# Second layer, latent attention: the division of the probabilities on GpSimd instead of VectorE

## The reference, cut to what matters

```python
def causal_attention(q, k, v):            # blocks of 128 queries
    sc = einsum('bqhd,bkhd->bhqk', q_blk, k) * scale
    sc = where(mask, sc, -inf)
    p = softmax(sc, axis=-1)
    return einsum('bhqk,bkhd->bqhd', p, v)

def memory_attention(q, mem_k, mem_v):
    sc = einsum('bshd,bmhd->bhsm', q, mem_k) / sqrt(HEAD_DIM)
    p = softmax(sc, axis=-1)
    return einsum('bhsm,bmhd->bshd', p, mem_v)

tok = causal_attention(q, k, v)
mem_out = memory_attention(q_mem, mem_kv[:, :, 0], mem_kv[:, :, 1])
y = concatenate([tok, mem_out], axis=-1) * silu(gate)
h = layer_norm(ALPHA * h + y @ w_out[layer], ln_g[layer], ln_b[layer])
```

## Time and profile before

| | us |
|---|---|
| runs of the kernel before, median (lowest to highest) | 3575.22 (3570.03 to 3576.9) |
| profiled execution, span | 3578.9 |
| PE busy | 3274.2 (91%) |
| PE weight loads busy | 2587.5 (72%) |
| DVE busy | 1949.7 (54%) |
| POOL busy | 1561.2 (44%) |
| ACT busy | 1156.5 (32%) |

### The profile page before, as it was taken

One profiled execution on the slowest core, in us unless ns is written; L12 is line 12 of the kernel. 1 busy time (PEld: TensorE's weight loads), 2 busy tenths in 40 slices (PEclk: granted clock), 3 DMA queues, 4 the chain that ended last, 5 costly groups with the idle time before them and its releaser, 6 DMA issues. The chain is left out here.

```text
span 3578.9 us, 45809 instructions
## 1 busy us (share of the span) xinstructions
PE 3274.2 (91%) x17652; PEld 2587.5 (72%) x17652; DVE 1949.7 (54%) x2824; ACT 1156.5 (32%) x2265; POOL 1561.2 (44%) x1195
## 2 busy tenths in 40 slices
PE   5888999999699999889999999999897999899796
PEld 2666787788598888667788878887674566676465
DVE  3278854545444455587733373338413887665736
ACT  4144432333333333332211021102223664144713
POOL 1114645455143441156666666666551001554332
PEclk9988869999899999899999999999996999999887
DMA  4335536232253442343333333334434321222112
GB/s 166 89 106 165 154 118 185 86 83 83 69 140 98 122 125 65 105 144 94 89 94 100 95 89 100 94 100 104 141 101 119 79 60 50 83 81 59 47 52 72
DMA packets 524317, 358.55 MB, mean 100 GB/s; under 512 B 92497, under 2 KB 477382, under 8 KB 524102
## 3 DMA queue, kind: packets, MB, share of 16 engines
q1 hardware_dynamic: 513446, 325.22, 31.6%
q0 software_dynamic: 4608, 16.78, 1.5%
q10 hardware_dynamic: 6048, 13.63, 1.1%
HBM read 276.85 MB, written 78.18 MB: 99 GB/s over the span
## 5 line engine op out<-in xcount | busy, mean ns | idle before, releaser
L2403 PE MATMUL psum<-place,place 128*128 128x512 f32 x2126 | 862.7, 406 | 80.5 <-POOL place L2381 33.5
L2404 PE MATMUL psum<-place,place 128*128 128x512 f32 x2126 | 843.1, 397 | 0.0
L2405 PE MATMUL psum<-place,place 128*128 128x512 f32 x2126 | 841.0, 396 | 0.0
L2379 POOL CAST place<-place 128x1024 fp32r<-128x1024 f32 (+3 forms) x302 | 304.7, 1009 | 1119.9 <-PE psum L2405 674.8
L2381 POOL TENSOR_TENSOR place<-place,place 128x1024 fp32r<-128x1024 f32 (+3 forms) x302 | 691.3, 2289 | 24.2
L2403 PEld LDWEIGHTS psum<-place,place 128*128 128x128 f32 x2126 | 408.7, 192 | 197.9 <-POOL place L2381 51.8
L2404 PEld LDWEIGHTS psum<-place,place 128*128 128x128 f32 x2126 | 408.9, 192 | 90.3 <-issue 7.5
L2405 PEld LDWEIGHTS psum<-place,place 128*128 128x128 f32 x2126 | 408.3, 192 | 87.6
L659 PE MATMUL psum<-place,place 128*128 128x512 f32 (+1 forms) x712 | 289.0, 406 | 22.1 <-issue 10.5
L660 PE MATMUL psum<-place,place 128*128 128x512 f32 (+1 forms) x712 | 273.7, 384 | 0.0
L661 PE MATMUL psum<-place,place 128*128 128x512 f32 (+1 forms) x712 | 273.5, 384 | 0.0
(11 more groups left out here) (325 smaller groups left out, 5592.1 us busy)
## 6 DMA issues: line engine op xcount, KB each, us to landing
place<-in_w_mlp_up SPq DMA_DIRECT2D x64, 512.0 KB, 4.0
place<-in_w_mlp_down SPq DMA_DIRECT2D x64, 512.0 KB, 3.9
place<-in_w_out SPq DMA_DIRECT2D x48, 512.0 KB, 4.0
chunked<-place SPq DMA_DIRECT2D x64, 320.0 KB, 3.6
place<-in_w_in SPq DMA_DIRECT2D x34, 512.0 KB, 5.8
solve<-in_w_ada POOLq DMA_DIRECT2D x32, 512.0 KB, 6.2
place<-in_lru_w_in SPq DMA_DIRECT2D x32, 512.0 KB, 3.8
place<-in_mla_w_in SPq DMA_DIRECT2D x30, 512.0 KB, 4.2
```

The costliest lines, as they stand in the source:

```text
L2379: nc.gpsimd.tensor_copy(hi, raw).then_inc(self.w_split, 1)
L2403: pe.matmul(ps, self.w_hi[:, j, k, :], hi, start=(k == 0), stop=False)
L2404: pe.matmul(ps, self.w_hi[:, j, k, :], lo, start=False, stop=False)
L2405: mm = pe.matmul(ps, self.w_lo[:, j, k, :], hi, start=False, stop=(k == kt - 1))
```

## The change

The half units' multiplication moves from DVE to POOL; DVE keeps the reciprocal, and waits before it until POOL has multiplied g - 2, since the reciprocals have two places. POOL's program in `rest` becomes: the multiplications of g = 0 to 111; the first two splits of the chain's weights; the multiplications of g = 112 to 127; then the chain's splits as before. `Recall` keeps the multiplication on DVE.

```diff
     DEPTH = PV = 2
+    POOL_DIVIDES = True
...
+    def gpsimd(self, pool):
+        for g in range(self.G):
+            p, rd = self.prob[:, g % 2, 0:self.blocks(g // 2) * P], self.st[g % 2][:, 3:4]
+            pool.wait_ge(self.rden, g + 1)
+            self.C.nc.gpsimd.tensor_scalar(p, p, rd, None, ALU.mult).then_inc(self.probs, 1)
+            yield
...
             dve.wait_ge(self.exped, g + 1)
+            if self.POOL_DIVIDES and g >= 2:
+                dve.wait_ge(self.probs, g - 1)
             nc.vector.reciprocal(rd, tot).then_inc(self.rden, 1)
-            dve.wait_ge(self.rden, g + 1)
-            ts(p, p, rd, None, ALU.mult).then_inc(self.probs, 1)
+            if not self.POOL_DIVIDES:
+                dve.wait_ge(self.rden, g + 1)
+                ts(p, p, rd, None, ALU.mult).then_inc(self.probs, 1)
...
     DEPTH = PV = 1
+    POOL_DIVIDES = False
...
         def _(pool):
-            alternate(only(LIN, HELD), chain.gpsimd(pool), None, None, None, None, lru.clear(pool))
+            division, weights = a.gpsimd(pool), chain.gpsimd(pool)
+            for g in range(a.G):
+                if g == a.G - 16:
+                    next(weights)
+                next(division)
+            alternate(only(LIN, HELD)[1:], weights, None, None, None, None, lru.clear(pool))
```

## The result

| | before | after |
|---|---|---|
| median of the runs, us | 3575.89 (3570.03 to 3576.9) | 3627.4 (3624.16 to 3636.06) |
| ratio after to before, 95% interval | | 1.0166 (1.0132 to 1.0199) |
| profiled execution, span, us | 3578.9 | 3634.2 |
| DVE busy, us | 1949.7 | 1894.2 |
| POOL busy, us | 1561.2 | 1760.4 |

The kernel is 51.5 us slower by the medians, 47 to 71 us by the interval of the ratio, where I forecast +2 us; the time lies above my range, which ended at 3597. DVE lost 55.5 us of work; POOL got 199.2 us more, where DVE had needed some 64 for the same multiplications.

A forecast was written before the change was run, and what follows sets the result against it. PE was taken to bound the kernel. From the profiled 3578.9 us, 0.0 for relief and lateness, -1.6 for the collision and +3.5 for the stall gave 3580.8; on the median, 3577 us, range 3571 to 3597.

The forecast's parts named there:

- What bounds the kernel: Latent pairs: PE sets the pace, busy 35.65 of 38.02 us, so edits elsewhere can win at most 2.37 us a pair.
- Part 1: Multiplication leaves DVE in latent pairs: about 8 us of DVE work freed a pair, but only 0 to 0.3 us credited.
- Part 2: GpSimd's multiplication priced like its cast, 1.04 us at 1024 columns; lateness and relief together zero, -0.3 to +0.5 us a pair.
- slack: Time from a division's end to its first transpose's weight load; 0.49 us at n = 8 (key blocks), second head.
- the middle case: Rival, also the middle price: GpSimd takes 1.72 us for 1024 columns, 2.2 us a pair lost; +16, 3591 us; chance 0.24.
- the subtraction's price: Rival: GpSimd's multiplication costs as much as its two-tensor subtraction, about 6.7 us a pair; +46, 3621 us; chance 0.10.
- Part 3: Sixth latent pair: GpSimd's splits no longer collide with a DVE division, 39.62 to 38.02 us, a gain of 1.6 us.
- Part 4: Start of last memory pair: two splits queued ahead of g = 112's division stall PE 3.5 us, bounded by 2.5 and 4.5.

The follow-up runs named there:

- e1: Changed kernel with POOL's multiplication replaced by a copy of the probabilities onto themselves, division left out, waits and order kept: 1.0060 of before, 3595.17 us.
- e7: e1 with the two weight splits taken apart, the first before g = 112, the second behind the last g: 1.0001 of before.
- e3: Changed kernel with POOL multiplying by the constant 0.5 instead of the column of reciprocals, division left out: 1.0154 of before.
- e4: Kernel before, division still on DVE, with GpSimd's first two weight splits held until the division of g = 111 is done: 1.0003 of before.
- e6: e4 with DVE's multiplication of g = 112 held until the two splits are done, all multiplications on DVE: 1.0064 of before.
- e5: Changed kernel with both weight splits moved behind all divisions, multiplication on POOL at full price: 1.0154 of before.
- e9: Changed kernel with the n = 8 multiplications back on DVE and the splits apart as in e7: 1.0089 of before.

## Why the prediction was wrong, point by point

- **What bounds the kernel.** Right. PE sets the pace, and 2.37 us of idle time a pair were all there was to win; none was won.
- **Part 1, the relief of DVE.** Right: DVE's share of a latent pair fell from 31.33 to 23.75 us, and with the price of the copy the pair lasted 38.08 us where it had lasted 38.02. I had put relief and lateness together at zero, from -0.3 to +0.5.
- **Part 2, the price.** This is the step that failed first. I took the cast's 1.04 us for 1024 columns because both read one tensor; the multiplication takes 2.85, above the upper bound of 2.41 from the subtraction. I had written that both ends stay in the range, and then left the upper one out of it. With 1.04 the latent pairs do what I said (e1, e7). The reading of slack was sound in the main: it said that n = 8 loses from about 1.2 us on, and at 1.89 us a pair lost 1.8 us, at n = 2, 3, 4 and 8 (the middle case gave 2.2 for 1.72). For the subtraction's price it gave 6.7 us a pair; e3, dearer still, shows 5.9 at full clock, so my sum was too high there, and which of its terms was is not shown. The rule of the Trainium skill (GPSIMD Engine Reference, section 4.1) that one input is roughly line-rate holds here for the copy (1.04 us at 1024 columns, against 0.753 on DVE) and not for the multiplication by a scalar (2.85 us). The warning of the same section against elementwise work on GpSimd was the better guide.
- **Part 3, the collision.** Right to 0.1 us: 39.62 to 38.02 (e4), 38.09 (e1). L1728 (L1739 after) was not stretched:

```profile
L1739 DVE TENSOR_TENSOR place<-place,place 128x512 fp32r<-128x512 f32 x16 | 11.1, 693 | 19.6 <-ACT place L1784 19.6
```

  By the rule of the Trainium skill (SBUF — State Buffer, "Who interferes with whom") on a DVE operation with two SBUF inputs, 0.69 us could have been lost each time. The trace does not show that loss: 8 of the 16 began while a multiplication was running on POOL, in its last 0.12 to 0.40 us, and still took 0.69 us, and the multiplications beside them took no longer than the others of their width (2.20 to 2.21 us at 768 columns). A longer overlap of the two no run has.
- **Part 4, the stall.** The second failure. As a wait it was near: 3.5 us forecast, 2.79 measured in e1 and 2.73 in e6. I priced it as itself. What it cost there is 15.0 us (e6), since the clock was at 0.50 for the rest of the pair, and PE's 23.0 us of work at full clock became 36.3. In the changed kernel the clock fell ahead of it, so that the same kind of loss, 16.3 us, came from the price of part 2 already (e5), and the wait itself was 1.01 us. The earlier trace rows had shown a pair of this kind at clock 0.50 (the first one), and I read it only as a place where nothing could be lost.
- **The range.** The middle price (3591) was inside, the subtraction's price (3621, chance 0.10) was outside by choice. The result lies even beyond that case: by e3 the price explains 5.9 us of the 7.4 to 8.8 by which the second to fifth latent pairs are longer, and the clock most of the rest (2.5 us in e3 at 0.93, less in the pairs at 0.96), and most of the 16.3 in the last memory pair. No rival held the clock.

## What to carry to other kernels

Price an operation that the trace has never shown on that engine from both sides, and do not pick the cheap side because the operand count agrees: of three one-pass operations on POOL with one tensor in and one out, the copy cost 1.04 us and the multiplication 2.77 and 2.85. Before a wait is put on PE's path, however short, look at the granted clock of similar work in the same trace; if it is at half clock anywhere, the price of a wait can be several times its length. Work that is queued on an engine which is about to join a chain has to be cut into pieces that fit the slack (e7), or put where nobody stands behind it (e4); neither helps where the engine's own price has lowered the clock already (e5, e9).

## What the runs showed of the hardware that I had not expected

- GpSimd multiplies 1024 columns by a column of scalars in 2.85 us, by a constant in 2.77, and by the same column written as a repeated second tensor in 1.89. The form with two inputs is the faster of these.
- One wait of 2.73 us of PE at clock 1.00 was followed by 0.50 for the 33.5 us that were left of the pair (e6). After waits of 1.34 and 1.42 us at n = 8 the clock fell in e3's third latent pair (0.93), and after 1.33 and 1.42 it did not in its fourth (1.00). What decides between these two stays open.
- A memory pair seldom returned to full clock, and never for long: the first pair is at 0.50 in all runs, and in the last one the clock came back in the changed kernel and in e5 alone (0.76 from 3025 to 3030 us in e5), for 3.4 and 6.8 us, and fell again. Latent pairs did return: the changed kernel's second one is at 0.96 in the mean. A guess, not tested, is that the short, dependent steps of n = 2 keep it down.
- The moment at which the clock rises in the first latent pair differs between executions of the same code. It was at 1.00 there in the changed kernel (41.46 us) and at 0.84 in e5 (44.99), 0.93 in e1 (38.00) and 0.82 in e7 (40.95), and the code of each two is the same up to there. So the changed kernel's small loss in this pair, against 40.22 before, says nothing of the change. Why the clock rose earlier I can't say from these runs.
